# A weight ring whose four places lie 4112 bytes apart in place of 4096

## The reference, cut to what matters

```python
def swiglu(x, w_gate, w_up, w_down):
    return (jax.nn.silu(x @ w_gate) * (x @ w_up)) @ w_down      # 1024 -> 2816 -> 1024

# block 1: swiglu FFN, three-branch attention mixer with gates, swiglu FFN, each followed by a layer norm
# block 2: gated delta rule + compressed/selected attention, gates, then
f = rmsnorm(h, norm_ffn_pre[i]) @ w_up[i]                        # 1024 -> 5632
f = causal_dwconv(f, conv_ffn[i]) + conv_ffn_b[i]
f = (jax.nn.gelu(f_gate) * f_val) @ w_down[i]                    # 2816 -> 1024
```

## Time and profile before

| | |
|---|---|
| time, median of 3 runs (lowest, highest) | 1179.03 us (1178.21, 1185.97) |
| the profiled execution | 1180.69 us |
| its span, first to last instruction | 1178.8 us |
| PE busy / PEld busy | 94% / 88% |
| POOL busy / ACT busy / DVE busy | 77% / 53% / 44% |
| mean granted PE clock | 0.976 |

### The profile page before, as it was taken

One profiled execution on the slowest core, in us unless ns is written; L12 is line 12 of the kernel. 1 busy time (PEld: TensorE's weight loads), 2 busy tenths in 40 slices (PEclk: granted clock), 3 DMA queues, 4 the chain that ended last, 5 costly groups with the idle time before them and its releaser, 6 DMA issues.

```text
span 1178.8 us, 22455 instructions
## 1 busy us (share of the span) xinstructions
PE 1112.3 (94%) x8040; PEld 1034.8 (88%) x8040; DVE 521.6 (44%) x939; ACT 626.1 (53%) x1004; POOL 910.1 (77%) x700
## 2 busy tenths in 40 slices
PE   6999999999999998999998899899999998999985
PEld 6999997998998897999997889899889797999974
DVE  2423115402335565723213547774655344465554
ACT  5444445554556766444444855554565564555563
POOL 6899996998552596999998599393335777999973
PEclk9999999999998999999999899999998989999998
DMA  6966664576331455666666366252223554666642
GB/s 242 332 199 197 196 191 149 160 207 202 111 108 54 126 172 162 186 200 205 196 189 190 109 211 184 87 161 73 77 85 118 178 177 145 182 195 193 197 146 70
DMA packets 52631, 193.40 MB, mean 164 GB/s; under 512 B 5840, under 2 KB 6096, under 8 KB 51920
## 3 DMA queue, kind: packets, MB, share of 16 engines
q1 hardware_dynamic: 50976, 184.57, 51.7%
q10 hardware_dynamic: 1584, 7.81, 1.7%
HBM read 191.31 MB, written 1.05 MB: 163 GB/s over the span
## 4 chain that ended last, share of the span: by engine, by line
POOL 51%; issue 31%; PE 14%; DVE 2%; POOLq 1%; ACT 0%; DVEq 0%; ACTq 0%
POOL weights_low L499 51%; PE banks L530 8%; PE acc L530 6%; POOLq L502 0%; DVE xs L1883 0%; DVE stat L1898 0%; DVE res L1896 0%; DVE res L1910 0%; POOLq L496 0%; DVE xs L1916 0%; DVE acc L1880 0%; DVE act_buf L1759 0%; ACT tmp L1466 0%; DVE hf L1767 0%; PE banks L655 0%
## 5 line engine op out<-in xcount | busy, mean ns | idle before, releaser
L499 POOL TENSOR_TENSOR weights_low<-ring,weights_high 128x512 fp32r<-128x512 f32 x696 | 909.9, 1339 | 250.1 <-ACT weights_high L1226 247.4
L1226 ACT CAST weights_high<-ring 128x1024 fp32r<-128x1024 f32 x348 | 361.4, 1048 | 233.8 <-PE banks L530 118.6
L530 PE MATMUL banks<-xT_high,weights_high 128*128 128x256 f32 x1488 | 417.4, 281 | 2.2 <-POOL weights_low L499 1.7
L530 PE MATMUL banks<-xT_low,weights_high 128*128 128x256 f32 x1488 | 413.5, 278 | 0.0
L530 PE MATMUL banks<-xT_high,weights_low 128*128 128x256 f32 x1488 | 413.2, 278 | 0.0
L530 PEld LDWEIGHTS banks<-xT_high,weights_high 128*128 128x128 f32 x1488 | 280.9, 189 | 6.8 <-issue 2.1
L530 PEld LDWEIGHTS banks<-xT_low,weights_high 128*128 128x128 f32 x1488 | 281.0, 189 | 2.3
L530 PEld LDWEIGHTS banks<-xT_high,weights_low 128*128 128x128 f32 x1488 | 280.7, 189 | 0.0
L1734 DVE TENSOR_TENSOR hf<-act_buf,banks 128x256 f32<-128x256 f32 x40 | 16.8, 420 | 221.9 <-ACT act_buf L1252 221.9
L530 PE MATMUL acc<-weights_high,hT_high 128*128 128x512 f32 x264 | 103.9, 394 | 4.7 <-POOL weights_low L499 3.6
L530 PE MATMUL acc<-weights_low,hT_high 128*128 128x512 f32 x264 | 104.1, 394 | 0.0
(11 more groups left out here) (345 smaller groups left out, 1612.5 us busy)
## 6 DMA issues: line engine op xcount, KB each, us to landing
ring<-in_stream SPq DMA_DIRECT2D x348, 512.0 KB, 3.7
rows<-in_big_rows ACTq DMA_DIRECT2D x3, 1024.0 KB, 7.4
rows<-in_big_rows ACTq DMA_DIRECT2D x3, 512.0 KB, 4.3
cst<-in_consts ACTq DMA_DIRECT2D x1, 1411.0 KB, 9.6
gates<-in_x_fm SPq DMA_DIRECT2D x2, 512.0 KB, 5.1
xs<-in_x_tm ACTq DMA_DIRECT2D x1, 1024.0 KB, 6.2
out<-xs SPq DMA_DIRECT2D x4, 256.0 KB, 2.1
p_in<-in_p_fm ACTq DMA_DIRECT2D x1, 256.0 KB, 2.7
```

The source lines that it names most:

```text
L499: last = nc.gpsimd.tensor_tensor(wlo[:, slot, hs], ring[:, slot, hs], whi[:, slot, hs].bitcast(F32), ALU.subtract)
L530: ins = nc.tensor.matmul(o, lhsT, rhs, start=start, stop=stop, **kw)
L1226: nc.scalar.copy(whi[:, ch % RING, :], ring[:, ch % RING, :]).then_inc(S["hi_ready"], 1)
```

## The change

`weights_high` and `weights_low` get four unused float32 after each place of 1024, so a place starts 4112 bytes after the one before (4112 = 64 x 64 + 16). Chunk c's high and low halves then begin 0, 16, 32 or 48 bytes past a multiple of 64, for c mod 4 = 0, 1, 2, 3. `ring`, the target of the DMAs, stays at 4096. A `fill_high` of 448 bytes is put between the two, and `fill_x` is 64 bytes shorter, so that `weights_low` starts 512 bytes later than before, `cst` to `res` 576 bytes later, and everything from `xT` on 512 bytes later: each of them keeps its offset within 64 bytes. No instruction, wait or semaphore is added or removed.

```diff
         ring = sb("ring", [RING, CB * P])
-        whi, wlo = pair("weights", [RING, CB * P])
+        whi = sb("weights_high", [RING, CB * P + 4], dtype=F32R)[:, :, 0:CB * P]
+        sb("fill_high", [112])
+        wlo = sb("weights_low", [RING, CB * P + 4], dtype=F32R)[:, :, 0:CB * P]
@@
         res = sb("res", [2, D])
-        sb("fill_x", [88])
+        sb("fill_x", [72])
         xT = pair("xT", [KD, T])
```

## The result

The changed kernel takes 1194.5 us, median of 3 runs (1194.28 to 1195.86). Against the kernel before the ratio is 1.0115 (95% interval 1.0081 to 1.0149; the plain quotient of the two medians of three, 1194.5 / 1179.03 = 1.0131, lies in it): slower by a bit more than 1%. That is inside the range of 1168 to 1205, but not the forecast, which was no change, and beyond the 1174 to 1190 that the forecast took in with its small costs. The profiled execution has a span of 1194.1 us, 15.3 more than before.

A forecast was written before the change was run, and what follows sets the result against it. PE was taken to pace the FFNs, with a thin reserve on POOL. All terms were 0: 1180.69 + 0 = 1180.7 us, stated as 1180, no change; small costs reach 1190. The range was 1168 to 1205.

The forecast's parts named there:

- small costs: Upper bounds on top of 1180.7 us: 7.8 for the moving operand and 1.3 for POOL, reaching 1190.
- What bounds the kernel: PE paces the FFNs, losing about 0.5 of 7.2 ns per 64-byte line; POOL's reserve is 0.15 us per chunk.
- Stationary operand from the ring, price 0: 4086 shifted weight loads on PE cost 0; at the very most 6 ns each, 24.5 us.
- Moving operand from the ring, 0 to 7.8 us: 1080 shifted matmuls on PE, one more line of 7.2 ns each at most; taken as 0.
- ACT, POOL, the other tensors, DMAs, waits, at 0: ACT's cast, POOL's subtraction, other tensors and DMAs cost 0, no wait changes; POOL at most 1.3 us.
- Rival: slower by the moving operand: PE's feed joins two lines per 64 bytes off the grid: 17.2 us more, 1198, or 247 more, 1428; chance 0.13.
- the runs of 12: Consecutive 512-column matmuls, 2.75 us in the third FFN; lengthening by place would show a price on the moving operand.
- the runs of 48: Consecutive 256-column matmuls, 5.47 us in the third FFN; lengthening would show a price on the stationary operand.
- Rival: slower by POOL: A shifted POOL stream takes twice as long, 0.43 us per instruction; FFNs cost 97 us more, 1278; chance 0.06.
- Rival: faster: PE's moving and stationary reads meet at one place of a line; shifting parts them, saving 29.8 us: 1151; chance 0.07.
- Rival: no other address: Ring slices laid out at the old pitch after all: 1180 us; only slopes by place could tell; no chance given.
- The pages: By the skill's 16-byte lines no operand touches one more line, term 0; by two independent PE read ports, no gain.

The follow-up runs named there:

- twelfth kernel: Kernel before with xT and the small tensors from stat to coef2 64 bytes later, ring and hT unmoved: 1197.28 us, ratio 1.0131.
- fifth kernel: Kernel before at its old pitch, with only the low half 512 bytes later and the tensors behind it 512 or 576: 1182.91 us, ratio 1.0022.
- tenth kernel: Kernel before with both halves of the ring and of xT 16 bytes later, all distances between them kept: 1179.25 us, ratio 0.998.
- ninth: Kernel before with the ring's halves, xT and all between them 64 bytes later, hT unmoved: 1186.14 us, ratio 1.0033.
- eleventh: Kernel before with a pitch of 4224, a stagger of 128 bytes for each place: 1182.94 us, ratio 1.0016.
- eighth kernel: The fifth kernel with the low half alone 64 bytes further, all places alike: 1196.66 us, ratio 1.0128 to the kernel before.
- sixth: Kernel before, old pitch, with all ring places 16 bytes on, xT's high half 16 and low half 80 bytes further: 1192.74 us, ratio 1.011.

## Why the prediction was right or wrong

The measured time lies inside the range, but by luck: the forecast (no change, with its small costs up to 1190) and its price of 0 for the stationary operand were wrong, and 1194.5 is covered only because the range had been drawn out to 1205 for a rival, a join of lines in the moving operand, which did not happen.

- *What bounds the kernel.* Right, and it is why the loss shows: PE sets the FFNs, and 15.3 of 20.8 us of slower pace reach the end. The hint that was read out of the pace, about 7.2 ns for each 64 bytes at either width, doesn't bear weight: 114.0 ns is the mean of chunks at 113.3 and 114.4, and in the twelfth kernel 256 columns take 119.9 ns while 512 stay at 229.0, so the two widths don't go in proportion. The reserve behind it is on POOL, which got idler.
- *Stationary operand from the ring, price 0.* This is the step that failed. Some 5386 of these matmuls lost 3.48 ns on average, 18.7 us, inside the bound of 24.5 that I gave and far from the 0 I took. That the bound held is luck too: it was made of the 6 ns by which the `rcs` loads scatter, which have nothing to do with what happened. Two rows misled me. The loads of `rcs` do take 104 to 110 ns at every offset, still so after the change, and the loads from `tmp` 192 like those from `dec`, but the duration of a load says nothing of the pace of a stream, since each lies beside other work: matmuls 114 and 119 ns apart both show 0.28 us. I had read the pace from the chain for the bound of the kernel, and then priced the edit by durations. The second mistake is in the question: I priced an address, and what counts is two addresses together. No row before could show it in the FFNs, but the part of the attention stage at 118 ns with the same kind of operands could have told that 114 is not a constant of this loop.
- *Moving operand from the ring, 0 to 7.8 us.* Mis-sized by little: 1.83 ns for some 1115 matmuls, 2.0 us.
- *ACT, POOL, the other tensors, DMAs, waits, at 0.* Right: 1046 for 1048 ns, 1334 for 1339, PE's wait for POOL 14.5 for 14.4; and the move alone (fifth kernel) has a ratio of 1.0022 (0.9995 to 1.005).
- *Rival: slower by the moving operand.* The sign was right, the place wrong: the runs of 12 hardly lengthened, the runs of 48 did, by which the text itself would tell that the stationary side has the price. The twelfth kernel shows that this sign can't tell the two sides apart: there of the operands only the moving `xT` has another address, and the runs of 48 lengthen most.
- *Rival: slower by POOL.* Didn't happen. With each chunk 0.07 us longer on PE (a body of 5.65 + 2.78 for 5.47 + 2.75, three chunks), POOL's reserve grew.
- *Rival: faster.* It had the nearest mechanism, the two reads of PE meeting at the same place of a line, and the opposite sign. Ring and `xT` were already apart, at the one distance (64 of 128) that holds the better rhythm; the stagger took three places in four off it. Its argument against itself, by durations of 276 to 283 ns, was as empty as mine.
- *Rival: no other address.* Excluded by the slopes by place.
- *The pages.* The Trainium skill (Advanced Engine Details and Errata, SBUF Cachelines) with lines of 16 bytes led to 0 for this change; measured is 1.15%, and since a shift by 16 in all operands costs nothing (tenth kernel) and one by 64 in one of them does (twelfth), neither a line of 16 bytes nor one of 64 explains it. The Trainium skill (SBUF — State Buffer, Who interferes with whom) has two independent read ports for PE; here PE's pace depends on where the two operands lie against each other, 113.3 or 118 to 120 ns. So in this stream it matters how the two are placed to each other; whether it is at those ports that they meet, no run shows.

What stays open: by what the two operands meet, as the runs only show that they do; distances other than 0, 48 and 64 of 128 (those of 32 and 16 occur only in staggered places, among others at other distances, and were slow there; 80, 96 and 112 occur nowhere); why kernels at the good distance still run some bodies at 117.8 (the ninth in turn, the eleventh one chunk in four, the fifth two FFNs of three, the kernel before in a part of attention, where the ninth and the tenth run at 114.0 and 114.2). That the spread of the kernel before over many runs (1177.04 to 1187.57 in 25, against 1.6 us for the changed one in 3) comes from whether a stage catches the better rhythm would fit, but only one run of each was profiled, and it isn't shown. Two things speak for another part in it: kernels that run at the slow pace throughout spread too (the twelfth from 1195.54 to 1202.08 in 4), and the longer runs tend to be those with the lower mean granted clock (the twelfth 0.976 in its longest and 0.981 to 0.982 in the others, the kernel before 0.981 in its shortest and 0.976 in its longest).

## What to carry to other kernels

When a PE-bound stream is laid out anew, look at where its stationary and its moving operand lie against each other in the low seven bits of their addresses: here 64 bytes apart was the only distance tried that allowed the better pace, without securing it, and a stagger in steps of 128 bytes was free where one of 16 or 64 cost 1.2 to 1.4%. Price an edit of a pipelined stream by the times between starts, for which durations are no stand-in, and look in every stage of the trace for the same loop at another pace before calling its pace a constant.

## What the runs showed of the hardware that I had not expected

- A stream of load and matmul pairs of 256 fp32r columns has two rhythms at the granted clock of 1.00: 113.3 ns and about 118 (up to 120, where the distance is wrong). The same program can have both, FFN by FFN (fifth kernel: 438 and 428 matmuls in 60 us).
- In these runs whole bodies had the better one only with the two operands 64 bytes apart modulo 128 and high and low halves alike: 113.3 to 113.4 ns (tenth kernel) against 119.7 to 120.1 with the moving one 64 bytes further (twelfth).
- Where both lie off a multiple of 64 bytes together, by 16, nothing is lost: ratio 0.998 (0.9959 to 1.0002). Where both are moved by 64, a little is: 1.0033 (1.0017 to 1.0049).
- One of three products at another position can slow all three (eighth kernel: 119.1 and 119.4 ns for those left in place, 116.4 for the moved one), though not always (sixth: 113.4, 117.5 and 122.5). In the time, a stagger of high alone has the ratio 1.0146, of low alone 1.0118, of both 1.0115.
- 512 columns with the ring as the moving operand feel little: 229.0 ns before, 229.8 to 232.8 after.
